# Mixer layers, the start and last state of an S5 core, and the output projection of sparse attention put in another order

## What is computed

```python
def first_block(x, mem, ...):
    h = x
    for l in range(2):
        h = h + hybrid_mixer(rms_norm(h), ...)
        h = h + memory_cross_attention(rms_norm(h), mem, ...)
    return rms_norm(h, norm_final)

def second_block(x, ...):
    h = x
    for layer in range(2):
        h = h + 0.5 * _swiglu(_rmsnorm(h), ...)
        u = _rmsnorm(h, mix_norm[layer])
        h = h + (_s5_mixer(u, ...) if layer == 0 else _nsa_mixer(u, kv, ...))
        h = h + 0.5 * _swiglu(_rmsnorm(h), ...)
        if layer == 0:
            kv = _shared_kv(h, ...)
    return h
```

```python
bu = einsum(u by groups of 16 channels, B)            # complex, 64 states
x[t] = A_bar * x[t-1] + bu[t]                         # a scan over the tokens
y = gelu(Re(x @ C) + D * u)
return y * sigmoid(y @ w_glu)
```

## Time and profile before

| | before |
|---|---|
| median of 3 runs | 1445.51 us |
| lowest and highest | 1441.36 and 1445.65 us |
| profiled execution, its own time | 1446.56 us |
| its span | 1444.8 us |
| mean granted TensorE clock | 0.989 |
| TensorE busy | 1396.4 us (97%) |
| VectorE busy | 853.1 us (59%) |
| ScalarE busy | 807.6 us (56%) |
| GpSimd busy | 337.2 us (23%) |
| read from HBM | 221.16 MB, 154 GB/s over the span |

### The profile page before, as it was taken

How to read it: one execution, slowest core, us unless ns; L and a number is a source line. 1 busy time by engine, 2 the same in 40 slices (tenths; PEclk the granted TensorE clock), 3 DMA queues, 4 the chain that set the end, 5 groups by cost and what they waited for, 6 DMA issues and landing times.

```text
span 1444.8 us, 22139 instructions
## 1 busy us (share of the span) xinstructions
PE 1396.4 (97%) x7389; PEld 1153.2 (80%) x7389; DVE 853.1 (59%) x1256; ACT 807.6 (56%) x1333; POOL 337.2 (23%) x377
## 2 busy tenths in 40 slices
PE   7998989999989999999999999999999999999998
PEld 6886878887777888877788888888888875788887
DVE  5537665446668567748655555645555678565553
ACT  7766476575665454544654444765444558554442
POOL 2011000011449999958300000010000015000000
PEclk9999999998999999989999999999999999999999
DMA  9532635530646555322876554677566310366661
GB/s 336 182 97 62 231 104 162 179 98 13 220 103 211 182 161 160 117 59 83 238 232 189 188 189 146 202 139 230 187 189 187 125 59 16 119 209 193 187 190 48
DMA packets 170862, 224.74 MB, mean 156 GB/s; under 512 B 14864, under 2 KB 114272, under 8 KB 170784
## 3 DMA queue, kind: packets, MB, share of 16 engines
q1 hardware_dynamic: 167984, 217.24, 47.8%
q0 software_dynamic: 2320, 6.18, 2.6%
q10 hardware_dynamic: 480, 0.29, 0.1%
HBM read 221.16 MB, written 1.44 MB: 154 GB/s over the span
## 4 chain that ended last, share of the span: by engine, by line
PE 74%; POOL 14%; DVE 6%; ACT 4%; issue 2%; DMA 1%; ACTq 0%; POOLq 0%; DVEq 0%
PE psum L1645 11%; PE psum L1633 8%; PE psum L1635 8%; PE psum L1634 8%; PE psum L392 8%; PE psum L394 8%; PE psum L393 8%; POOL arena L2007 4%; POOL arena L2006 3%; POOL arena L2005 3%; PE psum L530 2%; PE psum L418 2%; PE psum L539 1%; DVE w_lo L340 1%; PE psum L1672 1%
## 5 line engine op out<-in xcount | busy, mean ns | idle before, releaser
L1848 DVE TENSOR_TENSOR w_lo<-w_raw,w_hi 128x1024 fp32r<-128x1024 f32 x216 | 288.8, 1340 | 267.4 <-ACT w_hi L1771 267.1
L1771 ACT ACTIVATE w_hi<-w_raw 128x1024 fp32r<-128x1024 f32 x216 | 228.8, 1061 | 306.2 <-PE psum L1635 219.2
L340 DVE TENSOR_TENSOR w_lo<-w_raw,w_hi 128x1024 fp32r<-128x1024 f32 (+5 forms) x191 | 226.1, 1209 | 119.2 <-ACT w_hi L332 118.0
L1633 PE MATMUL psum<-w_hi,x_hi 128*128 128x512 f32 x704 | 280.0, 398 | 2.0 <-DVE w_lo L340 0.7
L1635 PE MATMUL psum<-w_hi,x_lo 128*128 128x512 f32 x704 | 274.8, 390 | 0.0
L1634 PE MATMUL psum<-w_lo,x_hi 128*128 128x512 f32 x704 | 274.2, 389 | 0.0
L332 ACT ACTIVATE w_hi<-w_raw 128x1024 fp32r<-128x1024 f32 (+5 forms) x191 | 192.8, 1038 | 102.5 <-PE psum L394 61.5
L392 PE MATMUL psum<-w_hi,x_hi 128*128 128x512 f32 (+6 forms) x608 | 230.7, 379 | 4.4 <-DVE x_lo L3000 2.3
L394 PE MATMUL psum<-w_hi,x_lo 128*128 128x512 f32 (+6 forms) x608 | 225.5, 371 | 0.0
L393 PE MATMUL psum<-w_lo,x_hi 128*128 128x512 f32 (+6 forms) x608 | 225.3, 371 | 0.0
L1633 PEld LDWEIGHTS psum<-w_hi,x_hi 128*128 128x128 f32 x704 | 132.3, 188 | 29.2 <-issue 2.2
(11 more groups left out here) (417 smaller groups left out, 1813.5 us busy)
## 6 DMA issues: line engine op xcount, KB each, us to landing
w_raw<-in_ffn_w_in SPq DMA_DIRECT2D x352, 256.0 KB, 3.2
w_raw<-in_ffn_w_out SPq DMA_DIRECT2D x176, 256.0 KB, 2.8
w_raw<-in_w_in SPq DMA_DIRECT2D x88, 256.0 KB, 3.6
w_raw<-in_w_out SPq DMA_DIRECT2D x32, 256.0 KB, 3.9
w_raw<-in_w_kv SPq DMA_DIRECT2D x24, 256.0 KB, 2.9
w_raw<-in_mem_wk SPq DMA_DIRECT2D x16, 256.0 KB, 5.6
w_raw<-in_mem_wv SPq DMA_DIRECT2D x16, 256.0 KB, 5.2
w_raw<-in_mem_wq SPq DMA_DIRECT2D x16, 256.0 KB, 6.5
```

Source lines behind the costliest of these rows:

```text
L340: nc.vector.tensor_tensor(w_lo[:, s, 0:size(u)], w_raw[:, s, 0:size(u)], w_hi[:, s, 0:size(u)].bitcast(F32), ALU.subtract).then_inc(lo_rea ...
L1633: nc.tensor.matmul(o, xh, whi, start=(kt == 0), stop=False)
L1771: nc.scalar.activation(w_hi[:, s, :], w_raw[:, s, :], ACT.Copy).then_inc(hi_ready, 1)
L1848: nc.vector.tensor_tensor(w_lo[:, s, :], w_raw[:, s, :], w_hi[:, s, :].bitcast(F32), ALU.subtract).then_inc(lo_ready, 1)
```

## The change

It changes the order of work and the engine that does it; all products are computed as before. A filler of two products more is added.

- **Mixers:** ScalarE lifts the latents before it converts the two units that stood ahead of them. VectorE makes the low parts of `uq` after the masked copies. Scores of latent attention wait for the heads of their own pair only; GLA's reciprocal root and one low part move from ahead of the attention into it, behind jobs 0 and 1.
- **Cross attention:** ScalarE copies query pair 0, VectorE pair 1, and scores wait for their own pair.
- **S5:** the hooks that turn C come one round of the feed-forward product later. Of the first half of `u` SyncE now issues six transfers, ScalarE three and GpSimd seven. Filler ahead of the first product is five, not three. For q = 7, the sine product and the real part's difference go to VectorE (`dve_last_state`); SyncE waits for GpSimd's product of q = 7 too before its fourth glu unit.
- **Sparse attention:** the first tile's `x_hi` and `x_lo` are made inside the attention, behind jobs 18 and 21; the output projection's first unit goes tile by tile, each tile waiting for its own half, and the second half of tile 1 is waited for after four of the eight inner tiles.

```diff
@@ mla_jobs, mem_jobs @@
-                        bias=bc(mask, 1, 2), slots=slots_first, ready=[f"mla{l}.qT2", f"mla{l}.kT2"], a=a, t=t))
+                        bias=bc(mask, 1, 2), slots=slots_first, ready=[f"mla{l}.qT{a}", f"mla{l}.kT{a}"], a=a, t=t))
...
-                        by_rows=False, late=None, bias=None, slots=slots_first, ready=[f"mem{l}.qT1"], a=a, t=t))
+                        by_rows=False, late=None, bias=None, slots=slots_first, ready=[f"mem{l}.qT{a}"], a=a, t=t))
@@ act_project, act_mla_up, act_mixer @@
-            hi_parts(act, chunk_end(name) + RING - 1)
+            hi_parts(act, chunk_end(name) + (RING - 1 if convert else 0))
...
-            hi_parts(act, chunk_end(f"uq{l}.1"))
+            hi_parts(act, max(chunk_end(f"uq{l}.1"), chunk_end(f"in{l}.6") + RING - 1))
...
-            act_project(act, l, 6)
+            act_project(act, l, 6, convert=False)
@@ dve_mixer @@
             dve_mla_lift(dve, l)
-            lo_parts(dve, chunk_end(f"uq{l}.1"))
...
-            dve_gla_e(dve, l, between={0: lambda: dve_mean(dve, f"mla{l}", 40 + 8 * l, 4, MLA_R, f"mla{l}.ckv.sq1"), 1: keys_ready})
+            def queries_ready():
+                lo_parts(dve, chunk_end(f"uq{l}.1"))
+                dve_mean(dve, f"mla{l}", 40 + 8 * l, 4, MLA_R, f"mla{l}.ckv.sq1")
+
+            dve_gla_e(dve, l, between={0: queries_ready, 1: keys_ready})
...
-            lo_parts(dve, chunk_end(f"ukv{l}.1") + 1)
-            dve_rstd(dve, f"gla{l}", 24 + 8 * l, 8)
-            dve_attend(dve, f"mla{l}.sm", mla_jobs(l), between={4: lambda: dve_mla_gate(dve, l, 0)})
+            dve_attend(dve, f"mla{l}.sm", mla_jobs(l),
+                       between={0: lambda: dve_rstd(dve, f"gla{l}", 24 + 8 * l, 8), 1: lambda: lo_parts(dve, chunk_end(f"ukv{l}.1") + 1),
+                                4: lambda: dve_mla_gate(dve, l, 0)})
@@ act_mem, dve_mem @@
-            heads_out(act, "act", f"mem{l}.q", xqT, MEM_H, P, f"mem{l}.qT")
+            heads_out(act, "act", f"mem{l}.q", xqT, MEM_H, P, f"mem{l}.qT", pairs=[0])
...
+            heads_out(dve, "dve", f"mem{l}.q", xqT, MEM_H, P, f"mem{l}.qT", pairs=[1])
@@ pool_s5 @@
-            move_u(pool, 0, U_MOVES[7:16], "s5v")
+            move_u(pool, 0, U_MOVES[9:16], "s5v")
...
+                    if q == KT - 1 and i:
+                        continue
...
+                if q < KT - 1:
+                    nc.gpsimd.tensor_tensor(c[:, 0, :, 1:NC4], c[:, 0, :, 1:NC4], s[:, 1, :, 1:NC4], ALU.subtract
+                                            ).then_inc(*done("s5_pool", f"s5.x{q}"))
+
+        def dve_last_state(dve):
+            q = KT - 1
...
+            nc.vector.tensor_tensor(s[:, :, :, 1:NC4], z, w, ALU.mult).then_inc(*done("s5_dve", f"s5.p{q}.1"))
+            dve.wait_ge(*when(f"s5.p{q}.0"))
+            dve.wait_ge(*when(f"s5.p{q}.1"))
+            nc.vector.tensor_tensor(c[:, 0, :, 1:NC4], c[:, 0, :, 1:NC4], s[:, 1, :, 1:NC4], ALU.subtract
+                                    ).then_inc(*done("s5_dve", f"s5.x{q}"))
@@ s5_hooks, drive in pe_s5 @@
-                hooks[1, n + 1] = lambda n=n: c(n)
+                hooks[2, n + 1] = lambda n=n: c(n)
...
-                    pe_busy(pe, b, 3)
+                    pe_busy(pe, b, 5)
@@ act_s5, dve_s5 @@
             act_norm(act, "s5n", 60, lambda t: f"ff0.h1{t}", ["s5.D31.o1"])
+            move_u(act, 0, U_MOVES[6:9])
             for f in (2, 3):
...
+            dve_last_state(dve)
             for k in (4, 5):
@@ U_DONE, sp_s5 @@
-        U_DONE = ((16 * 7, 16 * 9), (16 * 12, 16 * 4))
+        U_DONE = ((16 * 9, 16 * 7), (16 * 12, 16 * 4))
...
-                move_u(sp, a, U_MOVES[0:(7, 4)[a]])
+                move_u(sp, a, U_MOVES[0:(6, 4)[a]])
...
+                if u == 3:
+                    sp.wait_ge(*when("s5.p7.0"))
@@ pe_nsa, act_nsa, dve_nsa @@
-            pe.wait_ge(*when("nsa.lo11"))
-            pe_chunk(pe, "wo_nsa.0")
+            pe_chunk(pe, "wo_nsa.0", tiles_first="nsa.half", after={4: lambda: pe.wait_ge(*when("nsa.lo11"))})
...
+            act_attend(act, "nsa.sm", nsa_jobs(), between={0: compressed_turned, 18: lambda: heads_hi(0, 0), 21: lambda: heads_hi(0, 1),
+                                                           24: lambda: hi_parts(act, chunk_end("qg.2") + RING - 1)})
+            for x in range(2):
+                heads_hi(1, x)
```

More of the change, by code:

```diff
@@ L932, in dve_mem_kv, with act_project @@
             lo_parts(dve, chunk_end(f"memv{l}") + RING - 1)
-        def act_project(act, l, c):
+        def act_project(act, l, c, convert=True):
             name = f"in{l}.{c}"
@@ L2924, in compressed_turned, with heads_hi @@
                                          ).then_inc(*done("cmp_act", f"cmp.pT{t}", frees=(f"cmp.ptb{t}",)))
-            act_attend(act, "nsa.sm", nsa_jobs(), between={0: compressed_turned, 24: lambda: hi_parts(act, chunk_end("qg.2") + RING - 1)})
-            for t in range(T):
+            def heads_hi(t, x):
                 act.wait_ge(*when(f"nsa.sm.pv{16 * t + 15}"))
-                for x in range(2):
-                    nc.scalar.activation(x_hi[:, 4 * x:4 * x + 4, t * P:(t + 1) * P],
-                                         bank(f"nsa.o{t}{x}").rearrange("p (a k) -> p a k", a=4), ACT.Copy
-                                         ).then_inc(*done("nsa_act", f"nsa.hi{t}{x}"))
+                nc.scalar.activation(x_hi[:, 4 * x:4 * x + 4, t * P:(t + 1) * P],
+                                     bank(f"nsa.o{t}{x}").rearrange("p (a k) -> p a k", a=4), ACT.Copy
+                                     ).then_inc(*done("nsa_act", f"nsa.hi{t}{x}"))
+            act_attend(act, "nsa.sm", nsa_jobs(), between={0: compressed_turned, 18: lambda: heads_hi(0, 0), 21: lambda: heads_hi(0, 1),
+                                                           24: lambda: hi_parts(act, chunk_end("qg.2") + RING - 1)})
+            for x in range(2):
+                heads_hi(1, x)
             for f in range(2):
@@ L3002, in dve_nsa @@
                                             x_hi[:, 4 * x:4 * x + 4, t * P:(t + 1) * P].bitcast(F32), ALU.subtract
-                                            ).then_inc(*done("nsa_dve", f"nsa.lo{t}{x}", frees=(f"nsa.o{t}{x}",)))
+                                            ).then_inc(*done("nsa_dve", *([f"nsa.lo{t}{x}"] + ([f"nsa.half{t}"] if x != t else [])), frees=(f"nsa.o{t}{x}",)))
             def lift_ffn():
```

9 lines of the change are left out of this document (7 added, 2 removed).

## The result

| | before | changed |
|---|---|---|
| median, 9 runs each | 1445.05 us | 1435.72 us |
| lowest and highest | 1439.63 and 1446.13 | 1431.72 and 1439.44 |
| ratio | | 0.9942, 95% interval 0.9927 to 0.9956 |
| span of the profiled execution | 1444.8 | 1431.3 |
| its mean granted clock | 0.989 | 0.999 |

What follows compares the result with a forecast made beforehand. TensorE was taken as the bound, busy 97% of the span. From 1446.56 us, 6.4 of waits and 3.1 of clock gave 1437.1; the three-run median lies 1.05 lower, hence 1436.0 us, range 1430.5 to 1442.0.

Steps and rivals of the forecast that it cites:

- up-projections, two layers: Mixers: earlier latent lifts remove two TensorE waits, but the root limits the gain to 1.2 us per layer, 2.4 in all.
- latent attention's scores by pair: Latent attention, twice: scores start with the first key copy, VectorE work reordered; 0.1 us per layer, 0.2 in all.
- cross attention: Query copies shared by ScalarE and VectorE, so first scores start sooner; 0.5 us per layer, 1.0 in all.
- turns of C: S5 parameters: the later round removes TensorE's 1.52 us wait at L2156, hidden by GpSimd's table chain; costed at 0.
- transfers of u: S5 core: GpSimd issues seven instead of nine transfers, so the first half lands earlier; 0.9 us, bounds 0.2 and 1.6.
- last state: S5 core, q=7: two operations to VectorE; costed at 0 because ScalarE waits for a glu weight; bounds 0 and 1.6.
- output projection of sparse attention: Starting by tile cuts TensorE's 2.34 us wait to about 0.3; 1.9 us gained, bounds 1.0 and 2.3.
- I cost it at 0 [...] TensorE merely arrives earlier: S5 parameters: GpSimd's busy table chain hides the removed wait at the turns; without that cover, worth 1.5 us.
- At most the idle 0.6 us: Latent attention: VectorE is busy 10.30 of 10.89 us, so reordering the same instructions returns at most its idle time.
- the upper bound 1.7: Up-projections in the mixers: the gain in us if nothing but VectorE's queue counts; the lower bound was 0.5.
- The likeliest is that one of the two goes: Clock: one of two half-clock windows, in layer 1's attention or at 640.18, disappears; 3.1 us gained, total's chance 0.33.
- The slow rival: New stands before ukv, both layers, and before glu each bring a clock fall over dense matmuls; 1454.5 us, chance 0.04.

Runs made afterwards that it cites:

- e3: The kernel before with only the new order of the latent up-projections, on ScalarE and VectorE: 1440.99 us, ratio to before 0.9987.
- e10: The kernel before with only ScalarE's half of the new up-projection order, lifts ahead of the two conversions: 1442.93 us, ratio to before 0.9994.
- e1: The changed kernel with the turns of C hung in one round earlier again: 1433.59 us, ratio to before 0.9937.
- e8: e1 with all four operations of the last state on GpSimd again: 1432.83 us, ratio to before 0.9929.
- e4: The kernel before with only sparse attention's output projection begun by the first tile: 1440.35 us, ratio to before 0.9984.
- e2: The kernel before with only the turns of C one round later: 1442.99 us, ratio to before 1.0001.
- e9: The kernel before with all of latent attention's edit alone, scores by pair and VectorE's order: 1442.42 us, ratio to before 0.9997.
- e11: The kernel before with only VectorE's half of latent attention's edit, root and low part between the jobs: 1442.14 us, ratio to before 1.0009.

## Why the prediction was right, and where it was not

The total, the sign and the likeliest case came out. But the sum under it was 6.4 us of waits and 3.1 of clock, 9.5, and it is 4.2 (0.8) and, over the runs that list a clock, 3.5, so 7.7. That the median still fell within 0.3 us of the forecast is in part luck: the 1445.5 that I subtracted from was the median of three runs, 3.5 us above the 1441.99 of the 73 later ones. Term by term, in lengths at full clock except for the turns of C:

| term | forecast | measured | from |
|---|---|---|---|
| up-projections, two layers | 2.4 | 2.8 | e3, e10 |
| latent attention's scores by pair | 0.2 | -0.5 | 17.03 and 16.76 |
| cross attention | 1.0 | 1.0 | the wait of 0.83 became 0.34, twice |
| turns of C | 0 | -1.9 (1.1) | e1 against the changed kernel, by the fit |
| transfers of u | 0.9 | 0.6 | 9.50 to 8.89; by the medians of seven, 0.9 |
| first B product, against VectorE's first scaling | 0 | -0.2 | 0.48 to 0.72 |
| last state | 0 | 0 | e8 |
| output projection of sparse attention | 1.9 | 2.4 | e4 |
| sum | 6.4 | 4.2 | fit: 4.2 (0.8) |

The turns' row and the last column come from the same fit, so that the sums agree says less than it seems to. What does test the rows is e1, which has all of the change but the turns: the other rows add up to 6.1, and e1 is 6.1 us (0.9) below before. The row of the transfers is the weakest, since its stage varies by more than the gain.

**The step that failed** is "I cost it at 0 [...] TensorE merely arrives earlier". It does not arrive earlier. The wait of 1.52 us at L2156 lay inside TensorE's longer wait for f_lo, which VectorE's queue of low parts sets, 15.1 us after the start of GpSimd's chain in both kernels. The turns filled that wait; moved away, they leave it open (2.04 us), cost their own time later, and TensorE is 1.05 us late at the end of the product. The cover that I had counted on, GpSimd's chain, is there: it hides all but about 0.2 us of that, as long as no fall adds to it. But the move also changed the cover itself (180.48 us busy instead of 178.81 in e2), and in the changed kernel's profile a fall of the clock stood right behind the wait that it had opened and cost 1.6. Whether the move brings that fall is not shown: e2 has the same wait, of 2.03 us, and no fall there. I had looked for what hides the gain and not for what TensorE would wait for next, on the very line behind.

**Latent attention** was bounded wrongly. "At most the idle 0.6 us" gave a gain an upper bound and took zero as the lower. The same instructions in another order were not the same length: L340 began 0.78 us before GpSimd's L1171 ended and took 1.86 us instead of 1.21, and GpSimd's L1174, held up in turn, 2.41 instead of 1.54. The Trainium skill, SBUF — State Buffer, section SBUF: two separate sides, says that of a VectorE operation with two SBUF inputs and a GpSimd operation that reads SBUF the one that starts first holds the shared pair for its whole instruction, and the other is blocked. By that, as an estimate, L340 would run from 139.43 for 1.21 us, to 140.64, and L1174 from there for 1.54, to 142.18; the trace has 140.51 and 141.92, which agrees within 0.3 us. And the low part stood ahead of the larger jobs of the second tile.

**The up-projections** were right in mechanism: L1244 starts when the root does, and the root came 1.3 us earlier. That only VectorE's queue counts, the upper bound 1.7, was nearer than my deduction of half a microsecond for the squares. The new stand ahead of ukv is 0.79 to 1.00, and 0.53 stands ahead of uq, where I had 1.3 in one.

**Sparse attention**: no wait is left at all, and the 0.1 for ScalarE was not spent. VectorE's low parts of tile 0 stand behind its last job (L3028 at 1215.26 in the changed kernel), not between jobs as the description of the change has it, and still come in time. That is the 0.5 of difference.

**The clock.** "The likeliest is that one of the two goes" was about right in size (3.1 forecast, 3.5 by the means). The price of a fall was about right too: where one of 10.24 us covers the attention it takes 2.9 us more (2.4 and 2.5 in e1 and e8), where one covers the S5 core 3.2 (37.4 instead of 34.2 us from the first B product to the last scan; in e9 4.1). The reason I gave was thin, though. None of the four edits that were tried alone raised the clock: the mixers have 0.9922, the turns 0.9932, latent attention 0.9928, sparse attention 0.9932, and the kernel before 0.9928; e11, VectorE's half of latent attention's edit, has 0.9941. All together have 0.9957 to 0.9972, and taking latent attention's order out of them gives 0.9929 to 0.9938. Which combination does it stays open; cross attention and the transfers of u were not tried alone. The slow rival did not occur: behind the new stands ahead of ukv and glu no fall shows in the changed kernel's profile; the one fall stands behind the wait for f_lo, which no case of mine had.

So the answer is partly a cancellation: 3.1 us too much in four terms (2.6 of it in two), 0.9 too little in two others, a clock that gave a little more, and a starting point that lay high.

## What to carry to other kernels

When a step that waits is moved away, ask what its engine waits for next at the old place; work that stands inside a longer wait is free there, and moved it has to be hidden or paid for anew. Filler is no different: once the wait that it lay in has shrunk, it stands in the way. Put VectorE work with two SBUF inputs where GpSimd is idle and VectorE is too: with the same low part in the middle of the job list the attention took 1.7 us per layer more than with it behind the last job. And where the clock moves a kernel by ten microseconds from run to run, compare stages at full clock, or times at one mean clock, before crediting an edit.

## What was not expected of the hardware

One and the same kernel ran between clocks of 0.987 and 0.998, and 1436.8 to 1449.6 us, in 29 runs: 0.9% from end to end; at 0.93 us for each 0.001 of clock, about 10 of these 12.8 us lie in the falls. In the fourteen profiled executions falls came in lengths of 3.4, 6.8 and 10.2 us (the one at the very end of each left out), and all but one, the one at 445.62, at the same few places (latent attention of either layer, the start of the S5 core, its end and glu, sparse attention and its output projection), each in some executions and not in others. Stage lengths outside them mostly repeated within 0.05 us, but for the one that ends on the transfers of u.
